# One loop over turns 1 to 9 in the expert part of a two-layer decoder trunk, with the overflow part behind a branch in its body

## The chip, the core and the metric

The kernel runs on one core of a Trainium2 chip. The metric is the device time of one execution in microseconds (us). The kernel before took 1073.08 us (median of 3 runs, 1072.5 to 1073.57).

## The reference, cut to what matters

256 tokens of 1024 channels go through two layers in float32. Each layer has a mixer (layer 0: gated spatial mixing and stick-breaking attention; layer 1: a short gated convolution) and then a mixture of 32 experts, of which every token uses two. The experts are the part that the change touches.

```python
for l in range(DEPTH):                       # 2 layers
    x = x + mixer(rms_norm(x, norm_mix[l]))
    t = rms_norm(x, norm_ffn[l])
    # top-1 of 4 groups, then top-2 of the 8 experts in that group
    combine = sum(one_hot(expert_idx, 32) * weights, axis=1)
    for e in range(32):
        h = silu(t @ w_gate[e]) * (t @ w_up[e])          # 1024 -> 512
        out = out + combine[:, e:e + 1] * (h @ w_down[e])  # 512 -> 1024
    x = x + out
return rms_norm(x, norm_final)
```

Each expert has three matrices of 2 MB (gate, up, down), so 32 experts of two layers are 384 MB of weights that are read once.

## The kernel before

**An expert.** An expert works on the tokens that chose it, at most 32 of them (`CAP`). TensorE gathers them by a matmul with a selection matrix (`gather`, L1639), multiplies by gate and up (`gate_up`, L1610), scatters the result of the expert before (`scatter`, L1626), turns the weighted selection (`turn_wsel`, L1634), gathers for the next expert, and multiplies by down (`down`, L1617). ScalarE does the silu and two copies (L788 to L792), VectorE the product, two transposes, the gain and the next two selection matrices (L1229 to L1260). The results of all experts gather in four banks of PSUM.

**The weights.** They go through a ring of nine slots of 2 MB, which is three experts. SyncE issues every load. A slot is filled again when its matrix has been used: `gate_used`, `gu_ready` and `y_ready` are raised by TensorE when the gate, up and down product of an expert is done. Expert 2 of each layer (`EARLY`) has buffers of its own. Experts 3 to 11 and the last two are loaded as three transfers of 2 MB each (`second`, L424; the experts below `FINE = 12`), experts 12 to 29 as one transfer of 6 MB (`whole`, L430), issued when the down product of the expert three places earlier is done.

**Two kinds of count.** The 2 MB transfers are counted on nine semaphores `landed`, the 6 MB ones on three semaphores `whole_landed`. TensorE waits before every matrix in the first case and once before the gate matrix in the second.

**The turns.** A turn is three experts, so that the slots repeat and a loop over turns can be rolled. `TURNS` is 10, `MIDDLE` is 5. TensorE has expert 0 to 2 unrolled, a loop over turns 1 to 3 (L1756), a loop over turn 4 alone (L1759), the overflow part, a loop over turns 5 to 9 (L1765), and the last two experts unrolled (`last_experts`). ScalarE and VectorE have two loops each, cut at turn 5. SyncE loops over 6 MB loads, cut behind the loads of turn 5.

**The overflow part.** If an expert was chosen by more than 32 tokens, blocks of 32 further tokens are worked off apart, in `more_experts` (TensorE L1771, ScalarE L822, VectorE L1297) and `overflow` (SyncE L441). VectorE counts the blocks during expert 0 into a small table, `extra`. Every engine loads the sum of it into a register (L358) and jumps over the part if it is 0. Just before it TensorE adds the residual rows x to the four banks by 8 matmuls with the identity (`put_x`, L1376). `PAUSE` is the expert after which all this happens: 14.

Of the kernel before, what the change touches and what calls it, by code (L numbers as in the profile page):

```python
# [16 lines left out]
TT = S // P  # L17
# [6 lines left out]
NE = G * EG  # L24
# [23 lines left out]
RING_FIRST = (0, 1, 3)  # L48
MIDDLE = 5
PAUSE = MIDDLE * TRI - 1  # L50
SPARE_XG = 1
# [15 lines left out]
def entry(l, e):  # L67
    return L_MOE[l] + 3 * (e - (e > EARLY))


def place(n):
    return (n + 2) % RING
# [5 lines left out]

def is_whole(e):
    return FINE <= e < NE - 2  # L80


SINGLE = [z for z in SPLIT if z not in (L_EVEN, L_EVEN + 1, L_ODD)]
for layer in range(2):
    for expert in range(FINE):
        if expert != EARLY:
            SINGLE += [entry(layer, expert) + mat for mat in range(3)]
    SINGLE += [entry(layer, NE - 2) + mat for mat in range(3)]
    SINGLE += [entry(layer, NE - 1) + mat for mat in range(2)]
SINGLE.append(L_GAIN)  # L90
WHOLE = [(layer, expert) for layer in range(2) for expert in range(NE) if is_whole(expert)]


def single_count(n):
    return sum(z <= n and place(z) == place(n) for z in SINGLE)


def whole_count(l, e):
    return sum((zl, ze) <= (l, e) and place(entry(zl, ze)) == place(entry(l, e)) for zl, ze in WHOLE)

# [22 lines left out]
def trunk(nc, x_in, even_first, even_second, even_w_in, even_w_out, gmlp_w_s, gmlp_b_s, columns,  # L123
          odd_first, odd_w_in, odd_w_out, norm_gains, router, expert_weights_in, last_down, norm_final, out):
    with ExitStack() as ctx:
# [3 lines left out]
        def sem(name):  # L129
            return ctx.enter_context(nc.semaphore(name))  # L130
# [115 lines left out]
        landed = [sem(f"landed{i}") for i in range(RING)]  # L246
        whole_landed = [sem(f"whole_landed{i}") for i in range(RING // 3)]
        gate_used, out_half = sem("gate_used"), sem("out_half")
# [62 lines left out]
        def wide(n):  # L311
            return slot(n).rearrange("p (k f) -> p k f", k=K)

        def tall(n):
            return slot(n).rearrange("p (j d) -> p j d", j=4)
# [34 lines left out]
        def wait_landed(eng, n):  # L350

            eng.wait_ge(landed[place(n)], 16 * single_count(n))

# [26 lines left out]
        def _(sp):  # L380
# [49 lines left out]
            def whole(l, e, i, former):  # L430

                at = third(l, (i - 1) % TRI)
                sp.wait_ge(y_ready, after(l, former))
                sp.dma_start(ring[:, SLOT * 3 * at:SLOT * 3 * (at + 1)], expert_weights_in[l, e]).then_inc(whole_landed[at], 16)

# [33 lines left out]
            def experts(l):  # L469
# [20 lines left out]
                load_early(l, 1, 1, 2)  # L490
                for e in range(EARLY + 2, FINE):
                    second(l, e)
                for i in range(TRI):
                    e = FINE + i
                    whole(l, e, i, e - TRI)
                turns(l, ROLLED + 1, MIDDLE + 1)
                overflow(l)
                turns(l, MIDDLE + 1, TURNS)
                for e in LAST_TWO:
# [85 lines left out]
        def _(act):  # L585
# [218 lines left out]
            def moe(l):  # L804
# [8 lines left out]
                preload(ACT.Silu)  # L813
                for start, stop in ((0, MIDDLE), (MIDDLE, TURNS)):
                    with act.Fori(start, stop) as b:
                        for i in range(TRI):
                            expert(l, b * TRI + i)
                    if start == 0:
                        more_experts(l)
# [45 lines left out]
        def _(dve):  # L865
# [405 lines left out]
            def moe(l):  # L1271
# [12 lines left out]
                for i in range(TRI):  # L1284
                    expert(l, 0, i)
                    if i == 0:
                        more_blocks(l)
                for start, stop in ((1, MIDDLE), (MIDDLE, TURNS)):
                    with dve.Fori(start, stop) as b:
                        for i in range(TRI):  # L1290
                            expert(l, b, i)
                    if start == 1:
                        more_experts(l)
# [56 lines left out]
        def _(pe):  # L1350
# [340 lines left out]

            def apart_expert(l, T, i):
                n = entry(l, TRI + i)

                def wait_weights(mat):
                    pe.wait_ge(landed[place(n + mat)], (T + (single_count(n + mat) - 1)) * 16)

                expert(l, T * TRI + i, i, wait_weights, lambda mat: lambda k: wide(n + mat)[:, k, :], tall(n + 2))

            def whole_expert(l, T, i):  # L1700
                n = entry(l, FINE + i)

                def wait_weights(mat):
                    if mat == 0:
                        pe.wait_ge(whole_landed[place(n) // 3], (T + (whole_count(l, FINE + i) - ROLLED)) * 16)

                expert(l, T * TRI + i, i, wait_weights, lambda mat: lambda k: wide(n + mat)[:, k, :], tall(n + 2))
# [16 lines left out]
            def moe(l):  # L1724
# [26 lines left out]
                for e in range(TRI):  # L1751
                    if e == EARLY:
                        early_expert(l)
                    else:
                        first_expert(l, e)
                with pe.Fori(1, ROLLED) as T:  # L1756
                    for i in range(TRI):
                        apart_expert(l, T, i)
                with pe.Fori(ROLLED, MIDDLE) as T:  # L1759
                    for i in range(TRI):  # L1760
                        whole_expert(l, T, i)
                for t in range(TT):
                    put_x(t)
                more_experts(l)
                with pe.Fori(MIDDLE, TURNS) as T:  # L1765
                    for i in range(TRI):
                        whole_expert(l, T, i)
                last_experts(l)
# [85 lines left out]
```

## Time and profile before

| | before |
|---|---|
| median of 3 runs | 1073.08 us |
| profiled execution | 1073.68 us, its span 1071.9 us |
| mean TensorE clock granted | 0.894 |
| TensorE busy (matmul) | 815.4 us, 76% |
| VectorE, ScalarE busy | 315.0 us, 194.3 us |
| DMA | 439.94 MB, mean 410 GB/s |
| weight DMA in the chain that ended last | 50% |

The span is the time from the first to the last instruction of the profiled execution; 1.78 us of its own time lie around it. Durations in the rows below are from that execution. Busy time of TensorE is that of matmuls, which are pipelined. A float32 matmul of the program appears in the profile as two MATMUL and two LDWEIGHTS instructions, so that the 64 gate and up matmuls of one expert are "x128". The "DMA share" of a window is the mean busy share of the 16 DMA engines in it. "issue" as the releaser of a wait means that nothing which the profile shows ended it.

### The profile page before, as it was taken

The page shows a single profiled execution, that of the slowest core. Times are in us where ns is not written, and L with a number is a line of the kernel's source. Part 1 is how long each engine was busy: PE and PEld are TensorE (multiplying, and loading weights), DVE is VectorE, ACT ScalarE, POOL GpSimd, SP SyncE. Part 2 cuts the span into 40 slices and gives each one's busy share as a digit, 9 for nine tenths or more (in the row PEclk, how much of TensorE's full clock was granted, in tenths as well). Part 3 has the DMA queues.
Part 4 walks back from the last instruction along what each step waited for, and adds up shares of the span by engine and source line. Part 5 has one row for each costly group of instructions (what it writes and reads, how often), then busy time and mean ns, then how long its engine had stood idle before and what let it go on. Part 6 is the DMA issues. An engine that isn't in the chain of part 4 may idle for free.

```text
span 1071.9 us, 30246 instructions
## 1 busy us (share of the span) xinstructions
PE 815.4 (76%) x13956; PEld 648.5 (61%) x13957; DVE 315.0 (29%) x782; ACT 194.3 (18%) x363; POOL 5.4 (1%) x26
## 2 busy tenths in 40 slices
PE   9999889773867666676799998896565767666685
PEld 9788667552645445555599976564353545554563
DVE  5775422110111111111277744231111111111112
ACT  6784111000000000000254331110000000000002
POOL 1000000000000000000000000000000000000000
PEclk9999989887888888888999999998888888888889
DMA  9979999999999999999998599999999999999995
GB/s 374 424 297 375 422 425 429 427 437 435 429 430 429 437 428 437 431 435 419 418 429 341 219 398 424 426 427 429 440 429 435 426 430 435 433 433 431 435 419 241
DMA packets 25092, 439.94 MB, mean 410 GB/s; under 512 B 3008, under 2 KB 3520, under 8 KB 8384
## 3 DMA queue, kind: packets, MB, share of 16 engines
q1 hardware_dynamic: 24736, 438.36, 96.5%
q8 instruction: 58, 0.95, 0.4%
q10 hardware_dynamic: 288, 0.54, 0.1%
q14 instruction: 10, 0.08, 0.0%
HBM read 437.84 MB, written 1.05 MB: 409 GB/s over the span
## 4 chain that ended last, share of the span: by engine, by line
DMA 52%; PE 41%; issue 4%; DVE 2%; SPq 1%; ACT 1%; DVEq 0%; ACTq 0%
DMA ring<-in_expert_weights 50%; PE psum L1613 12%; PE psum L1399 8%; PE psum L1622 5%; PE psum L1472 4%; PE psum L1630 3%; PE psum L1642 3%; PE psum L1451 2%; DMA ring<-in_even_w_in 2%; PE psum L1636 1%; PE psum L1371 0%; PE psum L1358 0%; PE psum L1734 0%; PE psum L1523 0%; PE psum L1508 0%
## 5 line engine op out<-in xcount | busy, mean ns | idle before, releaser
L1613 PE MATMUL psum<-ring,m 128*32 128x128 f32 x7936 | 302.3, 321 | 222.6 <-DMA ring<-in_expert_weights 193.0
L1613 PEld LDWEIGHTS psum<-ring,m 128*32 128x32 f32 x7936 | 279.5, 131 | 253.2 <-issue 180.7
L1260 DVE TENSOR_TENSOR m<-psum,m 128x128 f32<-128x128 f32 x64 | 18.7, 292 | 548.1 <-ACT m L788 531.0
L1622 PE MATMUL psum<-ring,m 128*32 128x256 f32 x1984 | 123.1, 386 | 5.7 <-DMA ring<-in_expert_weights 3.9
L788 ACT ACTIVATE m<-psum 128x128 f32<-128x128 f32 x60 | 16.7, 278 | 495.9 <-PE psum L1613 495.9
L1399 PE MATMUL psum<-scr_halves,ring_halves 128*128 128x256 f32 x736 | 99.2, 284 | 0.4 <-ACT ring_halves L619 0.4
L1622 PEld LDWEIGHTS psum<-ring,m 128*32 128x32 f32 x1984 | 65.9, 112 | 53.1 <-issue 12.2
L1399 PEld LDWEIGHTS psum<-scr_halves,ring_halves 128*128 128x128 f32 x736 | 94.1, 192 | 1.0 <-ACT ring_halves L619 0.7
L1630 PE MATMUL psum<-m 32*128 32x256 f32 x1024 | 80.2, 416 | 11.0 <-issue 8.9
L1642 PE MATMUL psum<-x,m 128*32 128x256 f32 x1024 | 73.3, 405 | 2.0 <-issue 1.3
L1630 PEld LDWEIGHTS psum<-m 32*128 32x128 f32 x1024 | 49.7, 192 | 29.8 <-issue 23.9
L894 DVE TENSOR_TENSOR ring_halves<-ring,ring_halves 128x2048 fp32r<-128x2048 f32 (+1 forms) x32 | 63.6, 2022 | 12.9 <-ACT ring_halves L619 12.8
L619 ACT ACTIVATE ring_halves<-ring 128x2048 fp32r<-128x2048 f32 (+2 forms) x40 | 57.8, 1477 | 31.9 <-PE psum L1399 24.5
L1234 DVE STREAM_TRANSPOSE m<-psum 128x256 f32<-128x256 f32 x64 | 28.8, 450 | 106.3 <-PE psum L1642 106.3
L792 ACT ACTIVATE m<-psum 128x256 f32<-128x256 f32 x60 | 23.0, 384 | 158.4 <-PE psum L1622 158.4
L1642 PEld LDWEIGHTS psum<-x,m 128*32 128x32 f32 x1024 | 27.8, 113 | 26.1 <-issue 14.9
L1243 DVE TENSOR_SCALAR m<-count,pos,cw 128x128 f32<-128x128 f32 x128 | 38.3, 341 | 0.1
L790 ACT ACTIVATE m<-psum 128x256 f32<-128x256 f32 x60 | 23.0, 384 | 83.2 <-PE psum L1636 83.1
L1229 DVE TENSOR_SCALAR m<-count,pos,rstd 128x32 f32<-128x32 f32 x128 | 32.1, 295 | 2.1 <-issue 1.7
L1472 PE MATMUL psum<-ring_halves,aux_halves 128*128 128x512 f32 x96 | 32.7, 395 | 0.0
L1636 PE MATMUL psum<-ident,m 128*128 128x128 f32 x128 | 29.0, 309 | 0.0
L1237 DVE TENSOR_TENSOR m<-m,gains 128x256 f32<-128x256 f32 x64 | 27.2, 425 | 2.2
(196 smaller groups left out, 517.0 us busy)
## 6 DMA issues: line engine op xcount, KB each, us to landing
ring<-in_expert_weights SPq DMA_DIRECT2D x36, 6144.0 KB, 33.8
ring<-in_expert_weights SPq DMA_DIRECT2D x76, 2048.0 KB, 20.8
ring<-in_odd_w_in SPq DMA_DIRECT2D x5, 2048.0 KB, 27.0
ring<-in_even_w_in SPq DMA_DIRECT2D x3, 2048.0 KB, 22.4
ring<-in_even_w_out SPq DMA_DIRECT2D x2, 2048.0 KB, 31.6
spare<-in_expert_weights SPq DMA_DIRECT2D x2, 2048.0 KB, 21.2
ring<-in_last_down SPq DMA_DIRECT2D x8, 512.0 KB, 32.2
ring<-in_odd_w_out SPq DMA_DIRECT2D x2, 2048.0 KB, 29.6
```

What stands on the lines that cost most here:

```text
L619: act.activation(hi_slot(n)[:, c], raw_part(n, part), ACT.Copy).then_inc(w_hi, 1)
L894: dve.tensor_tensor(lo_slot(n)[:, c], raw_part(n, part), hi_slot(n)[:, c].bitcast(F32), ALU.subtract).then_inc(w_lo, 1)
L1229: last = dve.tensor_scalar(sel[:, t, CAP * i:CAP * (i + 1)], ranks, pos[:, bass.ds(at(e, t), 1)], rstd[:, t:t + 1], ALU.is_equal, ALU.mult)
L1234: return dve.transpose(xg[:, i, :, :], XB[:, 0:DP].rearrange("p (q k) -> p k q", k=K))
L1243: last = dve.tensor_scalar(wsel[:, t, :].rearrange("p (n c) -> p n c", n=NP), count[:, 1:CAP + 1].unsqueeze(1).to_broadcast([P, NP, CAP]), ...
L1399: return pe.matmul(bank[banks[c // 2]][:, (c % 2) * S:(c % 2 + 1) * S], w[a][:, k, P * c:P * (c + 1)], h[b][:, k, :], start=k == 0 and a + ...
L1472: last = pe.matmul(bank[2 * t + c][:, :], mix[a][:, 4 * r + j, P * t:P * (t + 1)], w[b][:, j, 512 * c:512 * (c + 1)], start=r == 0 and j = ...
L1613: last = pe.matmul(GU[CAP * part:CAP * (part + 1), lo:lo + FP], block_of(k), w_of(k)[:, FP * part:FP * (part + 1)], start=k == 0, stop=k = ...
L1622: last = pe.matmul(YB[CAP * part:CAP * (part + 1), 0:DP], h[:, CAP * f:CAP * (f + 1)], w[:, f, DP * part:DP * (part + 1)], start=f == 0, s ...
L1630: last = pe.matmul(bank[part][:, DP * t:DP * (t + 1)], cmb[r, P * t:P * (t + 1)], yy[r, :], start=first and t == 0, stop=False, skip_group ...
L1636: last = pe.transpose(BB[:, P * t:P * (t + 1)], wsel[:, t, :], ident[:, :])
L1642: last = pe.matmul(XB[CAP * part:CAP * (part + 1), 0:DP], sel[:, t, CAP * i:CAP * (i + 1)], x[:, t, DP * part:DP * (part + 1)], start=t == ...
```

## The change

One loop over turns 1 to 9 takes the place of TensorE's three, and of the two of ScalarE and VectorE. Its body ends with a branch, taken in turn 1 alone, that holds `put_x` and the overflow part on TensorE and the overflow part on the other two. `PAUSE` goes from expert 14 to expert 5. SyncE has its overflow part between the loads of expert 8 and expert 9, and one loop over the 6 MB loads of turns 5 to 9. So that one loop body can serve both sizes of load, the 6 MB loads are counted on the same nine semaphores: the transfer raises that of its first slot, and SyncE raises the other two by 16 just behind the issue. TensorE now waits before every matrix in every turn, the gate matrix first. Sizes, buffers and order of the loads stay.

```diff
-MIDDLE = 5
-PAUSE = MIDDLE * TRI - 1
+PAUSE = 2 * TRI - 1
...
-SINGLE = [z for z in SPLIT if z not in (L_EVEN, L_EVEN + 1, L_ODD)]
+COUNTED = [z for z in SPLIT if z not in (L_EVEN, L_EVEN + 1, L_ODD)]
 for layer in range(2):
-    for expert in range(FINE):
+    for expert in range(NE):
         if expert != EARLY:
-            SINGLE += [entry(layer, expert) + mat for mat in range(3)]
...
+            COUNTED += [entry(layer, expert) + mat for mat in range(3 - (expert == NE - 1))]
...
+def landed_count(n):
+    return sum(z <= n and place(z) == place(n) for z in COUNTED)
...
-                sp.dma_start(ring[:, SLOT * 3 * at:SLOT * 3 * (at + 1)], expert_weights_in[l, e]).then_inc(whole_landed[at], 16)
+                sp.dma_start(ring[:, SLOT * 3 * at:SLOT * 3 * (at + 1)], expert_weights_in[l, e]).then_inc(landed[3 * at], 16)
+
+                sp.sem_inc(landed[3 * at + 1], 16)
+                sp.sem_inc(landed[3 * at + 2], 16)
...
-                for e in range(EARLY + 2, FINE):
+                for e in range(EARLY + 2, 3 * TRI):
+                    second(l, e)
+                overflow(l)
+                for e in range(3 * TRI, FINE):
                     second(l, e)
...
-                turns(l, ROLLED + 1, MIDDLE + 1)
-                overflow(l)
-                turns(l, MIDDLE + 1, TURNS)
+                turns(l, ROLLED + 1, TURNS)
...
-                for start, stop in ((0, MIDDLE), (MIDDLE, TURNS)):
-                    with act.Fori(start, stop) as b:
-                        for i in range(TRI):
-                            expert(l, b * TRI + i)
-                    if start == 0:
+                with act.Fori(0, TURNS) as b:
+                    for i in range(TRI):
+                        expert(l, b * TRI + i)
+                    with act.If(b == 1):
                         more_experts(l)
...
-                for start, stop in ((1, MIDDLE), (MIDDLE, TURNS)):
-                    with dve.Fori(start, stop) as b:
-                        for i in range(TRI):
-                            expert(l, b, i)
-                    if start == 1:
+                with dve.Fori(1, TURNS) as b:
+                    for i in range(TRI):
+                        expert(l, b, i)
+                    with dve.If(b == 1):
                         more_experts(l)
...
+            def later_expert(l, T, i):
                 n = entry(l, TRI + i)
 
                 def wait_weights(mat):
+                    pe.wait_ge(landed[place(n + mat)], (T + (landed_count(n + mat) - 1)) * 16)
...
-                with pe.Fori(1, ROLLED) as T:
+                with pe.Fori(1, TURNS) as T:
                     for i in range(TRI):
-                        apart_expert(l, T, i)
-                with pe.Fori(ROLLED, MIDDLE) as T:
-                    for i in range(TRI):
-                        whole_expert(l, T, i)
-                for t in range(TT):
-                    put_x(t)
-                more_experts(l)
-                with pe.Fori(MIDDLE, TURNS) as T:
-                    for i in range(TRI):
-                        whole_expert(l, T, i)
+                        later_expert(l, T, i)
+                    with pe.If(T == 1):
+                        for t in range(TT):
+                            put_x(t)
+                        more_experts(l)
```

In the built program TensorE's stream has 15,211 instructions before and 10,462 after, if a float32 matmul is counted as four. The loop over turns 1 to 3 has 1192 of them; the new loop has 1679 from its head to its back edge, of which the branch jumps over 486 in turns 2 to 9. The new order has turn 1 to 9 as one body. On TensorE before, this is the end of the loop over turn 4 in layer 0, and the overflow part behind it:

```order
L1622 MATMUL psum<-ring,m 32x256 x16
L1759 REGISTER_ALU
L1759 COMPARE_AND_BRANCH
L1378 MATMUL psum<-x,ident 128x256 x8
L358 TENSOR_LOAD extra
L358 ISA x2
L371 COMPARE_AND_BRANCH
L1630 MATMUL psum<-m 128x256 x8
```

On TensorE after, this is the end of the third expert of the one loop (line numbers are lower in it), where L1739 is the new branch:

```order
L1611 MATMUL psum<-ring,m 32x256 x16
L1739 COMPARE_AND_BRANCH
L1367 MATMUL psum<-x,ident 128x256 x8
L345 TENSOR_LOAD extra
L345 ISA x2
L358 COMPARE_AND_BRANCH
L1619 MATMUL psum<-m 128x256 x8
```

And this is the end of the same loop body, with its back edge (L1736) and the first of the last two experts behind it:

```order
L349 COMPARE_AND_BRANCH
L1766 REGISTER_ALU
L358 UNCONDITIONAL_BRANCH
L1739 UNCONDITIONAL_BRANCH
L1736 REGISTER_ALU
L1736 COMPARE_AND_BRANCH
L1602 MATMUL psum<-ring,m 32x128 x64
```

The back edge stood right behind the third expert's down product and now stands behind the whole overflow code. On SyncE before, the loads of experts 4 to 17 of layer 0 stand ahead of the overflow part (L358 to L371):

```order
L382 DMA ring<-in_expert_weights 128x4096 x24
L434 DMA ring<-in_expert_weights 128x12288 x3
L437 UNCONDITIONAL_BRANCH
L434 DMA ring<-in_expert_weights 128x12288 x3
L437 REGISTER_ALU
L437 COMPARE_AND_BRANCH
L358 TENSOR_LOAD extra
L358 ISA x2
L371 COMPARE_AND_BRANCH
```

After, 15 of the 24 loads of 2 MB stand ahead of it, and this stands at its end:

```order
L358 UNCONDITIONAL_BRANCH
L369 DMA ring<-in_expert_weights 128x4096 x9
L421 DMA ring<-in_expert_weights 128x12288 x3
L427 UNCONDITIONAL_BRANCH
L427 ISA
```

The 9 loads of experts 9 to 11 and all 6 MB loads now stand behind the read of `extra` on SyncE's queue.

## Rows read from the trace of the kernel before

**Rows 1.** Page, part 2: 40 slices of the span, DMA share and rate.

```profile
PEclk9999989887888888888999999998888888888889
DMA  9979999999999999999998599999999999999995
```

**Rows 2.** Windows: engines' busy us, granted clock, DMA share, GB/s.

```profile
100.00:170.00 70.00, 61.41 (x1241) 45.41 (x1240) 27.22 (x104) 12.74 (x32) 0.00 (x0) 0.95 1.01 421
170.00:530.00 360.00, 247.95 (x5039) 190.24 (x5042) 62.95 (x200) 27.00 (x78) 0.00 (x0) 0.86 1.00 430
...
575.00:615.00 40.00, 40.00 (x306) 38.61 (x305) 28.56 (x33) 17.17 (x13) 0.00 (x0) 1.00 0.61 234
...
700.00:1035.00 335.00, 223.70 (x4558) 171.01 (x4550) 57.76 (x184) 24.43 (x70) 0.00 (x0) 0.85 1.00 431
```

**Rows 3.** Waits of TensorE: us in total, times, longest.

```profile
PE psum L1613 <- DMA ring<-in_expert_weights: 193.0, 47, 12.6
```

**Rows 4.** Source L434, the 6 MB loads, issue to landing.

```profile
DMA to landing us min/median/max: 24.8/33.8/42.1
```

**Rows 5.** Source L382, the load issued at 172.0 us, with its landing.

```profile
L382 SPq DMA_DIRECT2D ring<-in_expert_weights x1: 327/327/327, 172.0 to 172.0; - x1
DMA to landing us min/median/max: 26.6/26.6/26.6
```

**Rows 6.** Page, part 5: TensorE's scatter, 16 an expert.

```profile
L1630 PE MATMUL psum<-m 32*128 32x256 f32 x1024 | 80.2, 416 | 11.0 <-issue 8.9
```

**Rows 7.** Timeline of TensorE, layer 1, behind turn 4.

```profile
818.93 1.91 PE L1622 MATMUL psum<-ring,m 128*32 128x256 f32 x32
820.77 3.72 PE L1378 MATMUL psum<-x,ident 128*128 128x256 f32 x16
828.59 0.63 PE L1613 MATMUL psum<-ring,m 128*32 128x128 f32 x3 [4.11 <-issue]
835.44 5.25 PE L1613 MATMUL psum<-ring,m 128*32 128x128 f32 x125 [6.22 <-issue]
```

**Rows 8.** Page, parts 1 and 3: engines; queues, packets, MB, share.

```profile
PE 815.4 (76%) x13956; PEld 648.5 (61%) x13957; DVE 315.0 (29%) x782; ACT 194.3 (18%) x363; POOL 5.4 (1%) x26
...
q8 instruction: 58, 0.95, 0.4%
q14 instruction: 10, 0.08, 0.0%
```

**Rows 9.** Timeline of TensorE, layer 0: turn 1, its back edge at 170 us.

```profile
154.39 1.13 PE L1630 MATMUL psum<-m 32*128 32x256 f32 x12 [2.39 <-issue]
...
162.89 1.96 PE L1613 MATMUL psum<-ring,m 128*32 128x128 f32 x64 [0.84 <-issue]
...
169.40 0.62 PE L1622 MATMUL psum<-ring,m 128*32 128x256 f32 x3 [0.39 <-issue]
170.00 3.70 PE L1613 MATMUL psum<-ring,m 128*32 128x128 f32 x128
```

**Rows 10.** Timeline of TensorE, layer 0: experts 29, 30 and 31.

```profile
501.41 5.02 PE L1613 MATMUL psum<-ring,m 128*32 128x128 f32 x128 [5.01 <-DMA ring<-in_expert_weights]
...
508.69 1.91 PE L1622 MATMUL psum<-ring,m 128*32 128x256 f32 x32
510.41 3.68 PE L1613 MATMUL psum<-ring,m 128*32 128x128 f32 x128
...
517.61 1.95 PE L1613 MATMUL psum<-ring,m 128*32 128x128 f32 x64 [1.08 <-issue]
520.89 1.95 PE L1613 MATMUL psum<-ring,m 128*32 128x128 f32 x64 [1.32 <-DMA ring<-in_expert_weights]
522.77 2.27 PE L1384 MATMUL psum<-nones 128*128 128x128 f32 x18
525.81 0.42 PE L1622 MATMUL psum<-ring,m 128*32 128x256 f32 x4 [0.77 <-DMA ring<-in_expert_weights]
```

More of the change, by code:

```diff
@@ L76, in third @@
     return place(L_MOE[l] + 3 * i) // 3
-def is_whole(e):
-    return FINE <= e < NE - 2
-SINGLE = [z for z in SPLIT if z not in (L_EVEN, L_EVEN + 1, L_ODD)]
+COUNTED = [z for z in SPLIT if z not in (L_EVEN, L_EVEN + 1, L_ODD)]
 for layer in range(2):
-    for expert in range(FINE):
+    for expert in range(NE):
         if expert != EARLY:
-            SINGLE += [entry(layer, expert) + mat for mat in range(3)]
[L88 to L99, printed above, removed]
+            COUNTED += [entry(layer, expert) + mat for mat in range(3 - (expert == NE - 1))]
+COUNTED.append(L_GAIN)
+def landed_count(n):
+    return sum(z <= n and place(z) == place(n) for z in COUNTED)
 def pieces(n):
@@ L246, in trunk @@
         landed = [sem(f"landed{i}") for i in range(RING)]
-        whole_landed = [sem(f"whole_landed{i}") for i in range(RING // 3)]
         gate_used, out_half = sem("gate_used"), sem("out_half")
@@ L350, in wait_landed @@
         def wait_landed(eng, n):
-            eng.wait_ge(landed[place(n)], 16 * single_count(n))
+            eng.wait_ge(landed[place(n)], 16 * landed_count(n))
         @contextmanager
@@ L1690, in early_expert @@
                 expert(l, EARLY, EARLY, wait_weights, lambda mat: lambda k: halves[mat][k // HK][:, k % HK, :], spare)
-            def apart_expert(l, T, i):
+            def later_expert(l, T, i):
                 n = entry(l, TRI + i)
                 def wait_weights(mat):
[L1696 to L1705, printed above, removed]
+                    pe.wait_ge(landed[place(n + mat)], (T + (landed_count(n + mat) - 1)) * 16)
                 expert(l, T * TRI + i, i, wait_weights, lambda mat: lambda k: wide(n + mat)[:, k, :], tall(n + 2))
```

## The prediction

> **What bounds the kernel now.** I read the slices of the page first. After the first tenth of the span the DMA engines are at nine tenths or more everywhere but in slices 22 to 24 and the last one [rows 1]. Windows by stage say it exactly: from 100 us, where the experts of layer 0 start, the mean DMA share is 1.01 and then 1.00, at 421 and 430 GB/s, and it is 1.00 at 431 GB/s in layer 1; only between 575 and 615 us, in the convolution mixer, is it 0.61, since TensorE is busy there all the time (40.00 of 40 us) [rows 2]. So while experts run, the end is set by bytes over rate. The waits agree: TensorE stands 193.0 us for expert weights [rows 3].
>
> What a delay on TensorE costs is read from the queue of loads. A 6 MB load takes 33.8 us from issue to landing in the median and 24.8 at least [rows 4]; at 430 GB/s its own bytes are 14.6 us, so 19.2 us of earlier loads, 10.2 at least, lie ahead of it when it is issued. A delay of an issue is hidden as long as it is shorter than that. The 24.8 is itself the load behind the longest stall of TensorE (next part), so it is what remains after one.
>
> **The change part by part.**
>
> The overflow part does no work with these inputs: the scatter ran 1024 times, which is 16 for each of 64 experts and none for a further block [rows 6]. What is moved is the 8 matmuls of `put_x`, 3.72 us, the read of `extra`, and a jump over the overflow code. Behind them, in layer 1, TensorE stood 4.11 us, ran three instructions and stood 6.22 us more: from 820.77 to 835.44, 14.7 us in all [rows 7]. That now happens behind expert 5, at about 170 us in layer 0, instead of behind expert 14. What is queued behind it is gate and up of expert 6, which release the loads of expert 9. The load released at 172.0 us landed 26.6 us later [rows 5]; 4.9 us are its own (2 MB at 430 GB/s), so 21.7 us were ahead of it. 21.7 - 14.7 leaves 7 us: the queue does not run dry, and the move costs 0. What it gives back at turn 5 is also 0, since there 10.2 us remained. On SyncE the read of `extra` and its jump come behind the loads of expert 8 and run while TensorE does the same; the next issue waits for TensorE anyway. VectorE has written `extra` during expert 0. Without that cover the price would be 14.7 us a layer.
>
> The two more waits of TensorE for each of 36 experts, two semaphore increases for each 6 MB load on SyncE, and the register comparison at each turn's end on three engines are sequencer work of well under a microsecond each beside 193.0 us of waiting [rows 3]; I take 0. The trace before does not show an untaken branch at a loop's end; the bounds are 0 and the 4.11 and 6.22 us of a jump over code not seen before [rows 7], per turn, and both ends are hidden by the 10.2 us. The exception is the jump in turn 9, below.
>
> Code is fetched. The instruction queue that carries the most moved 58 packets, 0.95 MB [rows 8]. TensorE's stream has 15,211 instructions, so a packet holds 262 of them, and 58 packets are that stream once. It executed nearly 28,000 (13,956 matmuls and 13,957 weight loads) [rows 8]: loops were not fetched again. The timeline agrees. In turn 1 of layer 0 TensorE stops at 154.39, 162.89 and 169.40 us, each 126 or 127 matmuls (a packet's worth, weight loads counted) behind the last, and then passes the back edge at 170.00 with no gap at all and has no such stop in turn 2 [rows 9]. The new stream has 4749 fewer instructions, 18 packets. Their price: 0.4% of 1071.9 us over 58 packets is 0.074 us of all 16 engines each, together 1.3 us; by bytes alone at 430 GB/s it is 0.038 us each, together 0.7. I take 1.3, which is from the queue's own row. All 18 lie in the stretch where DMA is the limit, so they count in full.
>
> Against it stands the size of the body. The loop of before had 1192 instructions and stayed with the engine. The new one is 1679 from head to back edge, though 486 of them are jumped over: 6.4 packets, which touch 7 or 8. If the first is pushed out by what is fetched ahead at the end, one or two packets a turn come again, 16 in one layer: 1.2 us. No row says whether; I take half, 0.6 us, and keep 0 and 1.2.
>
> The Trainium skill (Runtime: NRT & Kernel Launch, Instruction fetch mechanics) has a rule for this: TensorE holds 2048 instructions in blocks of 256, filled in sequence. By it the new body still fits, barely, and the sum is the one here. The same section says that a taken branch to a block outside a window of two stalls for a fetch and that there is no cache. By that every back edge of 1192 instructions would have stalled; the trace disagrees, with a gap of 0 at 170.00 us [rows 9] and 58 packets for the run [rows 8].
>
> The sum against the profiled execution: 1073.68 - 1.3 + 0.6 = 1073.0 us. The median of the runs before lies 0.6 below that execution, so the forecast for a median is 1072.4 us, no change that can be measured.
>
> **The rivals.**
>
> *The body no longer stays with TensorE, and the kernel is slower.* The place is the loop of TensorE; it decides from the point where what the engine keeps is below the 7 to 8 packets of the body, and the trace shows only that it keeps the five or six of the old one. Then about 7 packets come again in each of 8 turns and 2 layers: 112 times 0.074 us is 8.3 us of DMA time. TensorE itself would have stops as in turn 1, up to 2.39 us a packet [rows 9]; five of them and three experts of at most 9.0 us (501.41 to 510.41) [rows 10] are 39 us, under the 43.8 us of three loads, and the queue hides the jump. The jump in turn 9 would not be hidden. Expert 30 starts right behind expert 29, at 510.41 us, and its slack to the down product at 525.81 is the waits of 1.08, 1.32 and 0.77 us, 3.2 in all [rows 10]. A stop of 4.1 to 6.2 us [rows 7] eats it and 1 to 3 us more, and the gate and up product of an expert takes 5.02 us behind an idle stretch instead of 3.68 [rows 10], so about 3 us a layer; the end of an expert part starts what comes next, so they count. Sum: 8.3 + 6 - 1.3 = 13 us, 1086 us if in both layers and 1079 if in one. For it: the size is 1.4 times the old. Against it: the body of before left no stop at all, which is not how a store looks that is nearly full, and the jumped part is not asked for. Chance 0.15.
>
> *The DMA queue runs dry behind turn 1, slower.* It needs the stop to grow from 14.7 to beyond 21.7 us. If the 10.3 us of standing doubled, it would be 25.0, and 3.3 us a layer would be lost: 1079 us. Rows 5 and 7 speak against it. Chance 0.04.
>
> *Fetching cost more than its share, faster.* A packet of code goes through fewer engines than a load does: the 0.4% is 68.6 us of one engine, 1.18 us a packet. If the packets fell on four of the 16 engines, every load would wait for those, and 18 packets fewer would save 18 * 1.18 / 4 = 5.3 us: 1068 us. The mean share of 1.00 over all engines [rows 2] speaks against it, but it would not show one per cent. Chance 0.10.
>
> *The change doesn't do what it says.* If the branch were taken in each turn, x would be added nine times, 3.72 us a time and hidden; that costs nothing in time and is not counted apart.
>
> **How the numbers follow.** The forecast has 0.71, with a range of its own of 1071.2 to 1073.9 (the fetch terms at their ends, and the 0.5 us by which runs differ). The rivals have 0.15, 0.04 and 0.10. A change under 0.2%, 2.1 us, can't be told from none by a measurement of this kernel. Nearly all of the forecast lies within it; of the third rival 0.02 as well, and small forms of it in the forecast go beyond: faster 0.11, same 0.71, slower 0.18. The range goes from 1069.5, between the forecast and the faster rival, to 1079, where the rivals in one layer end; it leaves out 1086 and 1068.
>
> **What would show it.** Right: instruction packets of the large queue fall from 58 to about 40 (to about 56 if a packet or two return each turn of one layer); DMA share stays 1.00 from 100 to 530 us; `put_x` at about 170 us with a stop of some 5 to 11 us behind it, and the load released next lands 12 to 22 us after its issue; expert 30 starts with no gap behind expert 29. Wrong: over 100 packets, stops at every 126 matmuls in turn 2 and later, or a gap before expert 30 of over 3.2 us; a window of 10 us with a DMA share below 0.9 between 170 and 210 us; or a rate above 435 GB/s in the same stretch, which the faster rival would bring.

## The result, and the profile after

The changed kernel is slower: 1127.76 us in the median of 6 runs (1125.74 to 1132.7), the kernel before 1073.01 (1072.17 to 1073.57) beside it, a ratio of 1.0515 with a 95% interval of 1.0505 to 1.0525. The forecast was 1072.4 and the range ended at 1079, so both missed.

The page of the changed kernel, its parts 1 to 4; the slices are to be laid beside [rows 1], the queues beside [rows 8]:

```profile
span 1124.9 us, 30438 instructions
PE 817.3 (73%) x13956; PEld 653.7 (58%) x13957; DVE 315.7 (28%) x782; ACT 194.3 (17%) x363; POOL 5.4 (0%) x26
...
PEclk9999898978888888888999999678696876869689
DMA  9979999999999999999985999997998989898991
...
q8 instruction: 112, 1.84, 0.7%
...
PE 58%; DMA 23%; issue 17%; DVE 1%; ACT 0%; SPq 0%; DVEq 0%; ACTq 0%
```

TensorE is busy for as long as before, 817.3 us against 815.4 [rows 8]. The DMA engines have tenths missing in the second part of the span alone, and the granted clock falls there too. The chain of work that ended last holds 17% of "issue", time in which TensorE waits for nothing that the profile shows. And where some 40 packets of instructions were foretold, there are 112.

The waits of TensorE (us in total, times, longest), beside the 193.0 us of [rows 3]:

```profile
PE psum L1602 <- issue: 167.6, 38, 14.7
PE psum L1602 <- DMA ring<-in_expert_weights: 104.1, 21, 11.7
```

Most of what was waiting for weights is now waiting for nothing visible. Windows by stage, columns as in [rows 2], say where:

```profile
170.00:530.00 360.00, 247.82 (x5050) 191.91 (x5045) 64.52 (x204) 26.82 (x77) 0.00 (x0) 0.86 1.00 431
700.00:1088.00 388.00, 229.12 (x4659) 174.35 (x4657) 60.20 (x192) 25.11 (x72) 0.00 (x0) 0.78 0.94 391
860.00:870.00 10.00, 10.00 (x215) 8.93 (x212) 2.50 (x8) 1.05 (x3) 0.00 (x0) 0.81 0.55 229
```

Layer 0 is what it was, a share of 1.00 at 431 GB/s. In layer 1 the share is 0.94 and the rate 391. In windows of 10 us the share falls to between 0.55 and 0.75 behind the heads of turns 3 and 5 to 8, and stays at 0.93 or more in turns 2, 4 and 9: the queue of loads runs dry in most turns. Nor is a load what ends last there any more. These are the longest waits of TensorE in the loop of layer 1, before (700 to 1040 us) and after (712 to 1090 us, where no wait for weights is left):

```profile
PE psum L1613 <- DMA ring<-in_expert_weights: 93.7, 22, 12.6
...
PE psum L1602 <- issue: 146.2, 26, 14.7
```

The timeline of TensorE (start, duration, operation, idle time before it and its releaser) shows the two layers apart. Layer 0, from the moved `put_x` into turn 2, and the back edge from turn 2 to turn 3:

```profile
171.65 3.72 PE L1367 MATMUL psum<-x,ident 128*128 128x256 f32 x16
...
179.18 6.26 PE L1602 MATMUL psum<-ring,m 128*32 128x128 f32 x128 [3.81 <-issue]
...
203.02 1.91 PE L1611 MATMUL psum<-ring,m 128*32 128x256 f32 x32
204.75 3.68 PE L1602 MATMUL psum<-ring,m 128*32 128x128 f32 x128
```

Layer 1, the same place, and then the heads of turns 3, 4 and 5, the head of turn 9, and what follows the loop:

```profile
696.82 3.72 PE L1367 MATMUL psum<-x,ident 128*128 128x256 f32 x16
711.92 2.34 PE L1602 MATMUL psum<-ring,m 128*32 128x128 f32 x34 [11.38 <-issue]
...
757.84 2.34 PE L1602 MATMUL psum<-ring,m 128*32 128x128 f32 x34 [13.19 <-issue]
763.29 5.17 PE L1602 MATMUL psum<-ring,m 128*32 128x128 f32 x94 [3.11 <-issue]
...
804.16 2.34 PE L1602 MATMUL psum<-ring,m 128*32 128x128 f32 x34 [13.76 <-issue]
...
852.99 2.34 PE L1602 MATMUL psum<-ring,m 128*32 128x128 f32 x34 [14.40 <-issue]
...
1049.94 2.34 PE L1602 MATMUL psum<-ring,m 128*32 128x128 f32 x34 [12.01 <-issue]
1056.77 5.20 PE L1602 MATMUL psum<-ring,m 128*32 128x128 f32 x94 [4.49 <-issue]
...
1093.08 4.35 PE L1602 MATMUL psum<-ring,m 128*32 128x128 f32 x101 [5.94 <-issue]
```

In layer 0 the back edge at 204.75 leaves no gap. In layer 1 every back edge leaves 11.4 to 14.7 us, and a second stop of 3.1 to 4.5 us follows 34 matmuls later. From 711.92 to 1049.94 are seven turns, 338.0 us, so 48.3 us a turn. The bytes of three loads need 43.8 by the estimate of the prediction; the kernel before took 301.9 us for the same seven turns, 43.1 each (rows below).

The kernel before, in the same places (head of turn 2 of layer 1, head of turn 9, expert 30):

```profile
699.75 3.67 PE L1613 MATMUL psum<-ring,m 128*32 128x128 f32 x128
...
1001.62 5.37 PE L1613 MATMUL psum<-ring,m 128*32 128x128 f32 x128 [4.11 <-DMA ring<-in_expert_weights]
...
1041.31 3.68 PE L1613 MATMUL psum<-ring,m 128*32 128x128 f32 x128
```

So the whole loss can be laid out. At the head of turn 2 the changed kernel is 12.2 us behind (711.92 - 699.75), in the seven turns to turn 9 it loses 36.1 more (338.0 - 301.9), and from there to expert 30 another 3.5 (1093.08 - 1041.31 is 51.8). The spans differ by 53.0. Nothing is lost ahead of the experts of layer 1: the first gate product starts at 641.15 us, before at 641.48.

The packets of code can be laid beside this, since the profile also counts those of queue 8 that start in a window. From 183 to 510 us, in turns 2 to 9 of layer 0, there is none. In layer 1 there are nine from the head of turn 3 to the head of turn 4 (757.84 to 804.16, the first line), and the second line is the stop before 757.84 alone (744.6 to 757.8):

```profile
q8 instruction: 9, 0.15, 1.5%
...
q8 instruction: 4, 0.07, 3.0%
```

These four are two pairs, two packets from 744.6 to 750 us and two from 750 to 757.8. So the stop at a head is not one fetch but two, one after the other. That they belong to the jump over the overflow code and to the back edge, the two taken branches at this place, is an inference.

**The theory to be tested (the first named, A or 1, in the expectations on this question).** TensorE keeps 8 packets of 256 instructions and fetches one ahead in order. So far this is a guess from the counts. A loop whose body touches 7 packets stays; one that touches 8 needs 9, the oldest is dropped each time, and all 9 come again in every turn. The count fits: a stream of 10,462 instructions is 40 packets, and 112 - 40 = 72 is 9 for each of 8 back edges of one layer. The body is counted as 1679 instructions, about 6.4 packets. Where it starts decides between 7 and 8. The stop in layer 1 comes 34 matmuls behind the head, which with their weight loads are 68 instructions, so the head lies 188 into its packet and the end, by an estimate of about 1650 for the body (the count is some 1 to 2% high: 262 counted to a packet of 256), some 46 into the eighth. In layer 0 the first border behind the head of turn 1 comes after 73 matmuls:

```profile
143.26 1.73 PE L1602 MATMUL psum<-ring,m 128*32 128x128 f32 x55 [0.64 <-issue]
```

So the head lies about 110 in (the expectations below take 106), and the end stays within the seventh. The rivals: the branch at the body's end or the new place of `put_x` is at fault, or the order of the other engines.

### The profile page after: what moved, and what is told of

The parts are those of the page before. It is cut to its first block, busy times and chain, and to the rows that moved or that the text cites. A ratio compares the mean times of both kernels' runs of the same rounds, so it can differ in the third digit from the quotient of the medians.

```text
span 1124.9 us, 30438 instructions
## 1 busy us (share of the span) xinstructions
PE 817.3 (73%) x13956; PEld 653.7 (58%) x13957; DVE 315.7 (28%) x782; ACT 194.3 (17%) x363; POOL 5.4 (0%) x26
## 4 chain that ended last, share of the span: by engine, by line
PE 58%; DMA 23%; issue 17%; DVE 1%; ACT 0%; SPq 0%; DVEq 0%; ACTq 0%
DMA ring<-in_expert_weights 23%; PE psum L1602 20%; PE psum L1388 9%; PE psum L1611 8%; PE psum L1619 5%; PE psum L1631 5%; PE psum L1461 4%; PE psum L1440 2%; PE psum L1625 2%; PE psum L1367 1%; PE psum L1373 1%; PE psum L1714 0%; PE psum L1360 0%; DMA gains<-in_norm_gains 0%; PE psum L1512 0%
## 5 line engine op out<-in xcount | busy, mean ns | idle before, releaser
L1602 PEld LDWEIGHTS psum<-ring,m 128*32 128x32 f32 x7936 | 279.3, 130 | 301.0 <-issue 250.7
L1611 PE MATMUL psum<-ring,m 128*32 128x256 f32 x1984 | 127.4, 388 | 1.4 <-issue 0.8
L1611 PEld LDWEIGHTS psum<-ring,m 128*32 128x32 f32 x1984 | 71.6, 112 | 42.1 <-issue 5.7
L1631 PE MATMUL psum<-x,m 128*32 128x256 f32 x1024 | 77.1, 394 | 13.9 <-issue 13.1
```

The lines of the kernel that those rows point to most:

```text
L1602: last = pe.matmul(GU[CAP * part:CAP * (part + 1), lo:lo + FP], block_of(k), w_of(k)[:, FP * part:FP * (part + 1)], start=k == 0, stop=k = ...
L1611: last = pe.matmul(YB[CAP * part:CAP * (part + 1), 0:DP], h[:, CAP * f:CAP * (f + 1)], w[:, f, DP * part:DP * (part + 1)], start=f == 0, s ...
L1631: last = pe.matmul(XB[CAP * part:CAP * (part + 1), 0:DP], sel[:, t, CAP * i:CAP * (i + 1)], x[:, t, DP * part:DP * (part + 1)], start=t == ...
```

## The experiments

**Only TensorE's loop cut in two.** All other engines keep the new order.

```diff
-with pe.Fori(1, TURNS) as T:
+with pe.Fori(1, 2) as T:
     for i in range(TRI):
         later_expert(l, T, i)
-    with pe.If(T == 1):
-        for t in range(TT):
-            put_x(t)
-        more_experts(l)
+for t in range(TT):
+    put_x(t)
+more_experts(l)
+with pe.Fori(2, TURNS) as T:
+    for i in range(TRI):
+        later_expert(l, T, i)
```

> The changed kernel with TensorE's loop alone cut again: turn 1, then put_x and the overflow part as straight code, then a loop over turns 2 to 9 (body about 1192 instructions). All other engines, the loads and the shared semaphores stay as changed, and the overflow part stays at turn 1. Theory A (instruction store: TensorE keeps 8 packets of 256 instructions and drops the oldest; a body that touches 8 of them, plus the one fetched ahead, is 9, and all come again each turn): 1071 to 1074 us, 48 to 52 packets on the large instruction queue, no stops in turns 3 and later. Theory B (the early place of the overflow part, or the counting on shared semaphores with two increases by SyncE, delays layer 1): still 1120 us or more.

Measured: 1071.75 us (10 runs), 0.9992 of before, interval 0.9983 to 1.0001. Its queue of code and its waits:

```profile
q8 instruction: 49, 0.80, 0.3%
```

```profile
PE psum L1602 <- DMA ring<-in_expert_weights: 199.6, 43, 12.5
PE psum L1602 <- issue: 29.9, 14, 4.7
```

The whole loss is gone: the waits are for weights again, as in [rows 3]. Everything that the change did on SyncE, ScalarE and VectorE, and the early place of `put_x` and of the overflow part, is still there. So it lies in TensorE's loop alone. This kernel is 5% faster than the changed one, and not told apart from the one before; none of these runs beat it by what can be measured.

**Layer 1's loop moved by 110 executed instructions**, put ahead of the wait for `chosen_ready`:

```diff
 keep_busy(6)
+for _ in range((0, 110)[l]):
+    pe.sem_inc(pad, 1)
 pe.wait_ge(chosen_ready, ...)
```

> The changed kernel with 110 semaphore increases on TensorE put in while it waits for the routing of layer 1. They only shift the place of layer 1's loop in the instruction stream: it starts about 42 instructions into a packet instead of 188, so its body touches 7 packets instead of 8. Theory A: layer 1 runs like layer 0, 1071 to 1074 us, packets fall from 112 to about 42. Theory B (early overflow, shared semaphores) and theory C (a taken jump over 486 instructions costs a stop in every turn of layer 1, wherever it lies): 1120 to 1130 us, packets about 112.

Measured: 1088.72 us, ratio 1.0147 (1.0133 to 1.0161). Code packets, and the timeline where the 110 stand:

```profile
q8 instruction: 40, 0.66, 0.2%
```

```profile
654.23 0.18 PE L1724 MATMUL psum<-chosen,below 128*128 128x32 bf16 x1 [13.83 <-issue]
```

The packets are back at 40 and no turn has a stop at its head, as the theory says. The time is 15 us over what it foretold, and this row says why: the increases themselves take 13.83 us, 126 ns each if nothing else lies in this stretch, on a part of the program where everything waits for TensorE. I had counted them as nothing. A cleaner form was needed.

**The same move by 110 instructions that never run**, in a branch that is never taken, inside a small loop so that it isn't decided beforehand:

```diff
 keep_busy(6)
+if (0, 110)[l]:
+    with pe.Fori(0, 2) as z:
+        with pe.If(z == 7):
+            for _ in range((0, 110)[l]):
+                pe.sem_inc(pad, 1)
```

> The changed kernel with 110 semaphore increases that never run, behind an untaken branch, in layer 1 ahead of its experts (a loop of two empty passes around them). They shift layer 1's loop in the stream as the last shift did, without the 14 us that running them cost. Layer 1's body touches 7 packets. Theory A (8 packets kept): 1070 to 1073 us, 40 to 42 packets. Theory B (early place or shared semaphores) and C (each taken jump stops layer 1): 1120 us or more.

Measured: 1073.68 us (11 runs), ratio 1.0006 (0.9997 to 1.0015).

```profile
q8 instruction: 40, 0.66, 0.2%
```

```profile
PE psum L1603 <- DMA ring<-in_expert_weights: 210.2, 47, 12.5
PE psum L1603 <- issue: 22.3, 11, 4.0
```

This settles the rivals that were left: body, branch, order and `put_x` are those of the changed kernel, and 54 us are gone when layer 1's loop starts 110 instructions further on, where by the count it touches 7 packets. It also has 18 packets fewer than before, and is no faster.

**Layer 0 moved into the bad place, layer 1 out of it**, 60 increases in layer 0 and 50 in layer 1 (the executed form, with `(60, 50)` for `(0, 110)`):

> 60 such instructions before the experts of layer 0 and 50 before those of layer 1. Layer 0's loop then starts 166 instructions into a packet (was 106) and touches 8 packets, layer 1's touches 7. Theory A: the slow turns move to layer 0: stops of 11 to 14 us at each turn's start there, none in layer 1, 1115 to 1130 us, about 112 packets. Theories B and C: the slow turns stay in layer 1.

Measured: 1096.05 us, one run, 76 packets (40 and 36), under the foretold 1115 to 1130 us and 112. The stops have moved to layer 0, and layer 1 has none. The heads of turns 5 and 6 of layer 0:

```profile
306.49 5.65 PE L1603 MATMUL psum<-ring,m 128*32 128x128 f32 x128 [5.12 <-DMA ring<-in_expert_weights]
...
360.89 2.76 PE L1603 MATMUL psum<-ring,m 128*32 128x128 f32 x43 [14.66 <-issue]
367.47 4.78 PE L1603 MATMUL psum<-ring,m 128*32 128x128 f32 x85 [3.81 <-issue]
```

The place is as foretold, the amount is half: stops of 11.6 to 16.0 us stand at the heads of turns 2, 4, 6 and 8 (that of turn 4 ends with a load of weights), 36 packets are 9 for each, and the turns between wait for their weights like any turn of before. That was not expected. The packets say the same turn by turn: none from 217 to 249 us and none from 297 to 347, nine from 347 to 392 and these from 249 to 297:

```profile
q8 instruction: 9, 0.15, 1.7%
```

Of the 23.4 us that this run is over the kernel before, up to 11.2 are the increases themselves, which run here too: TensorE stands 6.86 and 4.33 us where they are, 114 and 87 ns for each.

**Both layers in the bad place**, the executed form with `(60, 0)`:

> 60 such instructions before the experts of layer 0 alone. Layer 0's loop starts at 166, layer 1's at 248: both touch 8 packets. Theory A: both layers slow, 1165 to 1185 us, about 183 packets (72 more than with one). Theories B and C: 1120 to 1130 us.

Measured: 1173.97 us, one run, 148 packets: 40, 36 in layer 0 where again every second turn stops, and 72 in layer 1. The time fell within 1165 to 1185 by luck, with 35 packets fewer than foretold: layer 0 lost less, but the seven turns of layer 1 from 735.60 to 1095.79 us took 51.5 each instead of 48.3. Layer 1, turn 3:

```profile
784.13 0.64 PE L1603 MATMUL psum<-ring,m 128*32 128x128 f32 x4 [12.70 <-issue]
789.82 5.75 PE L1603 MATMUL psum<-ring,m 128*32 128x128 f32 x124 [5.05 <-issue]
```

The second stop now comes 4 matmuls behind the head instead of 34: 60 instructions further on, as the head was moved (30 matmuls with their weight loads). So the second stop marks the border of the head's packet. In turns 2 to 9 there is a third stop too, of 2.1 to 3.8 us at a later border.

**Layer 0 at two more places**, by never-run instructions: 110 in layer 0, `(110, 0)`, and 42 in layer 0 with 66 in layer 1, `(42, 66)`.

> The changed kernel with 110 instructions that never run ahead of layer 0's experts. Layer 0's loop starts about 220 instructions into a packet and ends about 90 into its eighth, layer 1's starts at about 45 and touches 7. With the loop of layer 0 at 166 every second turn stopped, 36 packets more. If that was because the body reached only 34 instructions into the eighth packet, all turns stop now: about 112 packets, 1120 to 1130 us. If it belongs to layer 0, every second turn stops again: about 77 packets, 1082 to 1092 us.

> 42 such instructions ahead of layer 0's experts and 66 ahead of layer 1's. Layer 0's loop starts at about 152 and ends about 20 instructions into its eighth packet; layer 1's touches 7. Theory A: at least every second turn of layer 0 stops, 76 packets or more, 1082 us or more; layer 1 has no stops. If the threshold were not at the packet's edge: 41 packets, 1071 to 1074 us.

Measured: 1145.98 us with 112 packets, and 1078.94 us with 73 (one run each). With 110 every turn of layer 0 stops, and the packets are as foretold, but the time is 16 us over the stretch: a turn takes 50.8 us (184.93 to 540.31 are seven), with a third stop of 2.0 to 3.9 us in a scatter. With 42 both numbers are under the foretold 76 packets and 1082 us. The stops stand at the heads of turns 2, 5, 7 and 9 (183.58, 305.48, 394.12 and 482.73 us), the last three with nine packets each and none between them, so that it isn't simply every second turn. Four stops cost 6.5 us here. Layer 1 has no such stop in either. Rows of both, the 110 first:

```profile
282.08 1.07 PE L1603 MATMUL psum<-ring,m 128*32 128x128 f32 x15 [12.76 <-issue]
287.81 5.34 PE L1603 MATMUL psum<-ring,m 128*32 128x128 f32 x113 [4.66 <-issue]
```

```profile
183.58 2.98 PE L1603 MATMUL psum<-ring,m 128*32 128x128 f32 x49 [11.78 <-issue]
```

In all runs the second stop gives the head's place in its packet, and head plus the 1650 of the body the end's, an estimate whose error wasn't measured: the body reaches 16 into its eighth packet with `(42, 66)` and 28 in layer 0 of the two runs with 60, and only some turns stop; it reaches 46 in layer 1 of the changed kernel, 84 in layer 0 with `(110, 0)` and 106 in layer 1 with `(60, 0)`, and every turn does.

**The kernel before, made to show the same.** Its loop over turns 5 to 9 gets code at its end that never runs:

```diff
 with pe.Fori(MIDDLE, TURNS) as T:
     for i in range(TRI):
         whole_expert(l, T, i)
+    with pe.If(T == 99):
+        for _ in range(450):
+            pe.sem_inc(pad, 1)
```

> The kernel before, with 450 instructions that never run behind a branch at the end of its loop over turns 5 to 9 of TensorE, in both layers. Nothing else of the change is in it. In layer 1 the body touches 8 packets, in layer 0 it touches 7. Theory A: stops of 11 to 15 us at the heads of turns in layer 1 alone, over 80 packets, 1082 to 1100 us. Theory B: as before, 1072 us, 62 packets.

> The same with 330 such instructions. In both layers the body touches 7 packets. Theory A: 1072 to 1074 us, about 60 packets. Theory C (a taken jump over hundreds of instructions costs a stop each time): the same as with 450.

Measured with 450: 1106.92 us, ratio 1.0326 (1.031 to 1.0342). With 330: 1073.99 us, ratio 1.0012 (1.0002 to 1.0021). The queue of code of the first and of the second:

```profile
q8 instruction: 98, 1.61, 0.6%
```

```profile
q8 instruction: 61, 1.00, 0.4%
```

And a head of a turn in layer 1, with 450:

```profile
935.84 2.34 PE L1614 MATMUL psum<-ring,m 128*32 128x128 f32 x34 [14.59 <-issue]
941.48 5.34 PE L1614 MATMUL psum<-ring,m 128*32 128x128 f32 x94 [3.31 <-issue]
```

A hundred and twenty never-run instructions make 33 us in a kernel that has nothing else of the change. With 450 there are 36 packets more than the some 62 of its stream (58 and 900 instructions more in two layers), 9 for each of the 4 back edges of this loop in layer 1, and all stops stand there (884.17, 935.84, 982.76 and 1030.85 us), none in layer 0. The time is 7 us over the expected stretch, since the stops here are at the upper end, 13.8 to 15.0 us, and 5.72 follow behind the loop. By the estimate of above this body reaches some 16 to 25 into its eighth packet, and yet every turn stops. So "a body that reaches only a few dozen instructions into its eighth packet stops in some turns alone" is no rule.

**How much of a stop is the traffic of the loads?** Each 6 MB load moves only its first quarter; the rest of a slot keeps older weights.

```diff
-sp.dma_start(ring[:, SLOT * 3 * at:SLOT * 3 * (at + 1)], expert_weights_in[l, e])
+sp.dma_start(ring[:, SLOT * 3 * at:SLOT * 3 * at + 3072], expert_weights_in[l, e][:, 0:3072])
```

> The changed kernel, in which each 6 MB load of experts 12 to 29 moves only its first quarter (1.5 MB); the rest of the slots keeps old weights. It tells what sets the length of the stops at the turns' heads in layer 1. If a fetch of code waits behind weight traffic, the stops of 11 to 14 us fall below 7 us from turn 4 on; if its time is its own, they stay. The number of packets stays about 112.

Measured: 930.6 us, one run, 112 packets again. A head of layer 1:

```profile
747.47 2.34 PE L1602 MATMUL psum<-ring,m 128*32 128x128 f32 x34 [10.28 <-issue]
750.78 4.52 PE L1602 MATMUL psum<-ring,m 128*32 128x128 f32 x94 [0.97 <-issue]
```

Neither expectation holds. The heads of turns 2 and 3, where the loads are still the whole ones, have 11.23 and 13.5 us as before. From turn 4 on, with the DMA engines at a share of 0.47, the first stop is still 9.96 to 10.54 us, where the changed kernel has 12.01 to 14.74, and the second goes from 3.1 to 4.5 down to 1.0 or less. So at this load about 10 us remain for the two fetches and what lies around them, and some 3 us of each of the two stops go with the traffic of the loads. What a stop would be with no load at all wasn't run.

**The overflow part ahead of the loop.** It leaves the loop on every engine, `put_x` and the overflow code stand behind expert 2, and no branch remains in the loop. TensorE's part:

```diff
+for t in range(TT):
+    put_x(t)
+more_experts(l)
 with pe.Fori(1, TURNS) as T:
     for i in range(TRI):
         later_expert(l, T, i)
-    with pe.If(T == 1):
-        for t in range(TT):
-            put_x(t)
-        more_experts(l)
```

> The changed kernel with put_x and the overflow part moved ahead of the loop on every engine, behind expert 2 (behind expert 5 on the changed kernel), so that no branch is in any loop and the body of turns 1 to 9 is 1192 instructions; SyncE has its overflow part behind the loads of expert 5. About 41 packets, every loop kept. Theory 1 (the queue of loads hides a stop only if it is longer): behind expert 2 only about 7 to 10 us of loads are ahead of the next one, put_x and the jump take 11 to 15 us, so the DMA share drops there and 2 to 6 us a layer are lost: 1074 to 1084 us. Theory 2 (the stop is hidden here too): 1070 to 1073 us.

Measured: 1081.43 us, ratio 1.0084 (1.0071 to 1.0098), 40 packets, within the stretch of theory 1. Windows of 5 us behind the moved part, layer 0 and then layer 1:

```profile
145.00:150.00 5.00, 3.96 (x76) 3.71 (x80) 0.00 (x0) 0.00 (x0) 0.00 (x0) 0.50 0.14 59
150.00:155.00 5.00, 5.00 (x98) 3.77 (x94) 0.70 (x2) 0.66 (x2) 0.00 (x0) 0.81 0.90 318
680.00:685.00 5.00, 3.85 (x80) 3.46 (x84) 0.00 (x0) 0.00 (x0) 0.00 (x0) 0.66 0.41 174
685.00:690.00 5.00, 5.00 (x114) 3.51 (x110) 1.54 (x5) 0.66 (x2) 0.00 (x0) 1.00 0.85 301
```

No code is fetched twice, and 9.0 us are lost all the same: at expert 2 the queue of loads is still short, and `put_x` with the stop behind it, 7.5 us from 138.56 to 146.04 in layer 0, empties it. The kernel before has a share of 1.00 or more in all four windows. The missing shares are 4.3 and 0.5 us in layer 0, 2.95 and 0.75 in layer 1, 8.5 together. This is the mechanism of the second rival, at a place three experts earlier than the change has it.

## Why the prediction was wrong

**The bound was read rightly, and for one layer only it stayed.** Layer 0 is bound by bytes as before. In layer 1 TensorE's turn of 48.3 us replaced the DMA's of 43.8.

**The step that failed** is the size of the body: "If the first is pushed out by what is fetched ahead at the end, one or two packets a turn come again, 16 in one layer". It is nine a turn, 72 in one layer. The second half of the step was to take their cost from the share of the DMA engines, 0.074 us each, and nothing for TensorE: the sum has 0.6 us there, and the runs show 53.0, since TensorE stands 11.4 to 14.7 us and 3.1 to 4.5 us in every such turn. A reading that fits: when what is touched in order is one packet more than what is kept, and the oldest goes first, each packet is dropped just before it is wanted again. In one turn nothing was seen between "stays" and "all again": even the runs with fewer stops have turns with 9 packets and turns with none. I had both numbers, "7 or 8" packets and one fetched ahead, and did not ask in which layer the body touches 8. Whether the order of the instructions could have told before a run is not shown: its count is 1 to 2% high, over thousands of instructions ahead of a head, and the body reaches in by only 46.

**The rule of the Trainium skill** (Runtime: NRT & Kernel Launch, Instruction fetch mechanics), that TensorE holds 2048 instructions in blocks of 256, is borne out by these runs as a size, 8 packets of 256. What I took from it, that the new body "still fits, barely", does not follow: by these runs what must fit is the packets touched, whole, and one more. In layer 0 that is 8, in layer 1 it is 9.

**The rival that came true was priced too low**, since it was judged like a single delay. Its own terms were 39 us for five stops and three experts, "under the 43.8 us of three loads, and the queue hides the jump". A queue hides a stop once. A stop in every turn belongs to the turn: 39 and the 10.3 us of standing behind a jump are 49.3, over 43.8 by 5.5, and eight turns make 44 us. Measured were 48.3 us a turn and 53.0 in all. So [rows 7, 9] give a number within 10 us of it, for the rival whose price I put at 6 us in one layer. This is in part luck, for the terms differ in kind from what was assumed: not five stops of 2.39 but one of 11.4 to 14.7 us and one of 3.1 to 4.5. Chance too is that the rival has a 112: there it is packets more, in both layers, and the page has 112 in all.

**The price of a packet for the DMA engines** came out as foretold and was beside the point: 0.7% of 1124.9 us over 112 packets is 0.070 us each, 0.074 foretold. The 54 packets more are 3.8 us of DMA time; TensorE's standing is the loss.

**The gain of 18 packets fewer**, 1.3 us, did not show: the kernel with 40 packets is at 1.0006 (0.9997 to 1.0015), which excludes it by a little unless something else in that kernel costs as much, and the one with 49 at 0.9992 (0.9983 to 1.0001), which doesn't. The third rival, 5.3 us faster, is excluded. (The upper end of the forecast's own range, 1073.9, comes out of its terms as 1074.1; nothing hangs on it.)

**What was right.** The early place of `put_x` and of the jump costs nothing. `put_x` stands at 171.65 us, foretold at 170. Behind it the stop is 3.81 us in layer 0, under the foretold 5 to 11; in layer 1 it is 11.38, which is the first of the recurring stops. From the start of `put_x` to the next gate product are 7.5 us, half of the 14.7 that the prediction took, and the load released next, at 182.9 us, landed after 14.2, foretold 12 to 22. The kernel with TensorE's loop cut has all of the moved work at the new place and 0.9992 of the time. The cover of the queue was weighed rightly too: at expert 5 it holds, at expert 2 it is short by 8.5 us of DMA time in both layers. The new waits, the semaphore increases of SyncE and the comparison at each turn's end are free, since the kernel shifted by never-run code has them all. The last jump behind turn 9 leaves no gap in layer 0, as the forecast had it (expert 30 starts at 507.54 us right behind expert 29). In layer 1 it isn't hidden, as the rival had it, and stops for 5.94 us, foretold 4.1 to 6.2; the expert it precedes is 3.5 us later against turn 9's head.

**What stays open.** Why some bodies that touch an eighth packet stop in every turn and others in every second or third one; three runs with a reach of 16 to 28 instructions in layer 0 skip turns and one with 16 to 25 in layer 1 does not, so the theory as stated, "all come again each turn", does not hold for all of them. Those three are single runs. How the 10 us of the first stop, which the traffic of the loads doesn't explain, divide is seen in part: two pairs of packets, one after the other. That the oldest packet is dropped is inferred from 9 for each stop and from the border between 7 and 8, and was not seen by itself.

## What to carry to other kernels

Count a loop body in whole packets touched, with the code that is jumped over and with where its head falls, and leave room for the one fetched ahead; a body at the limit can be right in one copy and wrong in the next. Compare the page's packets of instructions with the stream: once is good, more means that a loop comes again each turn. And weigh a stop that recurs against the slack of one turn, never against the queue alone: four stops with free turns between them cost 6.5 us here, eight in a row 53. Rare code belongs between loops, not in a body, and at a place where the queue of loads is long enough to cover it: ahead of the loop it cost 9.0 us, behind turn 1 none. Never-run instructions ahead of a loop are a cheap test for all of this: if the time moves, it is the place of the code.

## What the runs showed of the hardware that was not expected

- 110 instructions that never run took 54 us off one kernel, and 120 others (450 against 330) put 33 us on another.
- A semaphore increase that TensorE does execute takes about a tenth of a microsecond (stops of 13.83, 6.86, 5.63 and 4.33 us where 110, 60, 60 and 50 stand, 87 to 126 ns each); a hundred of them on the path are no neutral filler.
- Most of a stop at a back edge stays when the traffic falls: at a DMA share of 0.47 it is 9.96 to 10.54 us instead of 12.01 to 14.74.
- In such a stop two pairs of packets are fetched one after the other (two from 744.6 to 750 us, two from 750 to 757.8), and nine packets in the whole turn.
